# Pooling maps folded into the output projection, in a fused attention, pooling and ConvGLU block

## The reference

```python
h = rms_norm(x, norm1_g)                          # x: 2048 x 1024
q, k, v, p = split(h @ w_in)                      # 512, 128, 128, 512 columns
a = sliding_window_sink_attention(rms_norm(q), rms_norm(k), v, sinks)
for g, w in enumerate((2, 4, 8, 16)):             # four groups of 128 channels
    mixed = trailing_mean(p_g, w) - p_g           # divided by min(pos + 1, w)
    m_g = (mixed @ pool_w[g] + pool_b[g]) * pool_scale_g
x = x + concat([a, m]) @ w_out                    # 1024 x 1024
h2 = rms_norm(x, norm2_g)
u = h2 @ w_up                                     # 5632 columns
c = causal_depthwise_conv3(u) + conv_b
x = x + (silu(gate) * val) @ w_down
```

## Time and profile before

| | us |
|---|---|
| median of 3 runs | 1775.23 |
| the three runs | 1778.28, 1775.23, 1774.47 |
| the profiled execution | 1774.17 |
| its span, first to last instruction | 1772.4 |
| TensorE busy in it | 1758.5 (99%) |
| VectorE, ScalarE, GpSimd busy | 1289.6, 811.0, 251.5 |

### The profile page before, as it was taken

The page is one execution under the profiler, slowest core; times in us unless marked ns, Lnnn a source line. Parts: engine busy times, 40 slices in busy tenths (PEclk is TensorE's granted clock), DMA queues, the critical chain, the costliest instruction groups (busy, mean ns, idle before and its releaser), DMA issues.

```text
span 1772.4 us, 23447 instructions
## 1 busy us (share of the span) xinstructions
PE 1758.5 (99%) x8518; PEld 1465.8 (83%) x8518; DVE 1289.6 (73%) x1750; ACT 811.0 (46%) x1438; POOL 251.5 (14%) x272
## 2 busy tenths in 40 slices
PE   8999999999999999999999999999999999999999
PEld 7788888888878888888888888888888888888887
DVE  5645644635779888888888888888887778865774
ACT  4554644534665444444454444444444433333321
POOL 2222211202110000000000000000003033210210
PEclk9999999999999999999999999999999999999999
DMA  8653382484545524322376222223227999976884
GB/s 326 228 214 107 126 321 88 167 297 155 173 160 205 175 89 135 122 88 91 119 249 214 72 89 90 72 87 92 72 87 244 340 339 330 313 253 217 298 285 131
DMA packets 211557, 321.75 MB, mean 182 GB/s; under 512 B 13738, under 2 KB 106098, under 8 KB 211442
## 3 DMA queue, kind: packets, MB, share of 16 engines
q1 hardware_dynamic: 192014, 267.75, 45.2%
q10 hardware_dynamic: 19427, 52.49, 7.6%
HBM read 249.93 MB, written 70.25 MB: 181 GB/s over the span
## 4 chain that ended last, share of the span: by engine, by line
PE 96%; ACT 1%; DVE 1%; DMA 1%; POOL 1%; issue 0%; SPq 0%; ACTq 0%
PE ps L827 31%; PE ps L829 31%; PE ps L828 31%; PE ps L986 1%; PE ps L997 1%; PE ps L1050 1%; PE ps L1010 1%; POOL ss_q L2052 0%; DMA raw<-in_w_in_dram 0%; PE ps L973 0%; ACT xs L1251 0%; DMA x_d<-r 0%; PE ps L896 0%; DVE hT_lo L1582 0%; POOL w_lo L2074 0%
## 5 line engine op out<-in xcount | busy, mean ns | idle before, releaser
L827 PE MATMUL ps<-va_hi,wv 128*128 128x512 f32 x1232 | 479.7, 389 | 1.6 <-DVE va_lo L1769 1.4
L829 PE MATMUL ps<-va_hi,wv 128*128 128x512 f32 x1232 | 479.3, 389 | 0.0
L828 PE MATMUL ps<-va_lo,wv 128*128 128x512 f32 x1232 | 479.3, 389 | 0.0
L827 PEld LDWEIGHTS ps<-va_hi,wv 128*128 128x128 f32 x1232 | 231.3, 188 | 50.7 <-issue 2.3
L829 PEld LDWEIGHTS ps<-va_hi,wv 128*128 128x128 f32 x1232 | 231.3, 188 | 48.1
L828 PEld LDWEIGHTS ps<-va_lo,wv 128*128 128x128 f32 x1232 | 231.3, 188 | 47.7
L827 PE MATMUL ps<-dt_hi,ds_hi 128*128 128x512 f32 x616 | 239.6, 389 | 0.0
L828 PE MATMUL ps<-dt_lo,ds_hi 128*128 128x512 f32 x616 | 239.6, 389 | 0.0
L829 PE MATMUL ps<-dt_hi,ds_lo 128*128 128x512 f32 x616 | 239.6, 389 | 0.0
L1856 DVE SCALAR_TENSOR_TENSOR cb<-ub,cst,cb 128x1024 f32<-128x1024 f32 x176 | 218.9, 1286 | 9.1 <-ACT cb L1377 9.1
L1377 ACT ACTIVATE cb<-ub,cst 128x1024 f32<-128x1024 f32 x88 | 109.2, 1244 | 158.1 <-DVE ub L1905 94.6
(11 more groups left out here) (173 smaller groups left out, 2782.3 us busy)
## 6 DMA issues: line engine op xcount, KB each, us to landing
dg<-gT_d SPq DMA_DIRECT2D x264, 256.0 KB, 5.6
rw<-in_w_up_dram SPq DMA_DIRECT2D x84, 512.0 KB, 5.1
dw<-in_w_down_dram SPq DMA_DIRECT2D x132, 256.0 KB, 5.6
gT_d<-cb ACTq DMA_DIRECT2D x44, 512.0 KB, 2.6
raw<-in_w_out_dram SPq DMA_DIRECT2D x32, 512.0 KB, 4.0
w_hi<-wA_d SPq DMA_DIRECT2D x30, 512.0 KB, 3.4
w_lo<-wA_d SPq DMA_DIRECT2D x30, 512.0 KB, 4.8
n<-in_x_dram SPq DMA_DIRECT2D x16, 512.0 KB, 7.4
```

What stands on the lines that cost most here:

```text
L827: pe.matmul(out_ap, l_hi, r_hi, start=first, stop=False, skip_group_check=True)
L828: pe.matmul(out_ap, l_hi, r_lo, start=False, stop=False, skip_group_check=True)
L829: return pe.matmul(out_ap, l_lo, r_hi, start=False, stop=last, skip_group_check=True)
```

## The change

Before block 0's first `q` unit the four pool_w are turned on PE, scaled by pool_scale and split (`pwt`). Four new units `wp` in block 0 load the lower half of w_out, split it as any unit, and multiply it by the turned pool_w; ACT copies the eight 128x512 products out and stores them to DRAM (wP_d). `o` units k < 2 read wP_d in place of w_out. `pm` is gone in all blocks, with the splits in `win`. The bias row: SP loads the lower half of w_out once more into r (`bias_load`), POOL multiplies each of four rows by the bias and sums (`bias_sum`, seven passes over 128x1024), `bias_halves` splits the sum, PE sums over the partitions with a matrix of ones in block 1 (`bias`, four matmuls), ACT copies the row out (bias_all), and POOL adds it to the residual rows of every block before they are used (`rb`, four passes over 128x1024 a block). Block 0's residual rows are loaded later (`r_load`), since r holds the weights till then. The rest are orders: in blocks 1 and 2 the second `t1` part goes between `sp` 0 and 1; in the last block o(0,1) is cut into three pieces around the attention, `t2` takes other banks and waits, the second `va` loads and `va(0,2)` go later, and in up unit 0 the halves c = 0 go first, `hi(1,0)`/`lo(1,0)` go ahead, and the last `t2` pairs go into the middle of product 4.

```diff
@@ attention_order
+        if not back:
+            units("pwt", a, ())
         units("q", a, (0,))
-        units("pm", a, (0,), (1,))
+        if a == 1:
+            units("bias_halves", a, ())
         units("win", a, (2,))
...
         units("q", a, (1,))
+        if a == 1:
+            units("r_load", a, ())
         units("win", a, (3,))
         if more:
             units("n1sc", a + 1, ())
         units("q", a, (2,))
-        units("pm", a, (2,))
+        if a == 1:
+            units("bias", a, ())
+        if not back:
+            units("wp", a, (0, 0))
         units("q", a, (3,))
...
             units("t1", a + 1, (0,))
-            units("pm", a, (3,))
+            units("wp", a, (0, 1))
             units("t1", a + 1, (1,))
...
-            units("s", a, (0,), (1,))
+            units("bias_load", a, ())
+            units("s", a, (0,))
+            units("bias_sum", a, (0,))
+            units("s", a, (1,))
...
             units("inv", a, (1,))
+            units("bias_sum", a, (1,), (2,), (3,))
...
             units("av", a, (0,), (1,))
+            units("wp", a, (1, 0))
             units("sp", a, (2,), (3,))
...
             units("av", a, (2,), (3,))
+            units("wp", a, (1, 1))
             units("kve", a + 1, ())
             continue
+        units("rb", a - 1, ())
         units("o", a - 1, (0, 0), (0, 1))
...
     units("n2sq", last - 1, ())
+    units("rb", last, ())
     units("o", last, (0, 0))
     units("av", last, (0,), (1,))
-    units("o", last, (0, 1))
+    units("piece", last, (0,))
     units("sp", last, (2,), (3,))
     units("pt", last, (2,), (3,))
     units("n2sc", last - 1, ())
+    units("piece", last, (1,))
     units("av", last, (2,), (3,))
+    units("o", last, (0, 1))
     units("first_weights", last, ())
     units("t2", last - 1, (0,))
     units("o", last, (0, 2))
@@ SP
+            def r_load(a):
+                sp.wait_ge(S["bias_step"], 7)
+                sp.dma_start(r[:], x_v[:, 0:NT, :]).then_inc(r_in[0], 16)
@@ PE
+            def wp(a, n, h, pair):
...
+                for k in range(2):
+                    g = 2 * pair + k
+                    wait(pe, "fold_copied", 2 * (u - 1) + k + 1)
+                    mm = passes(ps[:, 4 + k, :], pw_hi[:, g, :], pw_lo[:, g, :], hi[:, k, :], lo[:, k, :], True, True)
...
                 if a == 1 and g < 2:
-                    pe.wait_ge(S["m_copied"], 3 + g)
+                    pe.wait_ge(S["fold_copied"], 3 + g)
...
+                        if dt < 2:
+                            pe.wait_ge(S["PT_ready"], NT * NB - 1 + dt)
+                        else:
+                            pe.wait_ge(S["aT_lo"], NT * NB - 3 + dt)
@@ ACT
             def first_weights(_):
                 act.wait_ge(S["spread_done"], NT * NB)
-                act.wait_ge(S["pool_done"], 4 * NB)
+                act.wait_ge(S["r_ready"], NT * NB)
                 for i in range(NP):
                     hi(0, i)
@@ DVE
             def o(a, n, h, k):
...
                 for t in range(NT):
+                    if h == 0:
+                        dve.wait_ge(S["r_ready"], NT * a + t + 1)
@@ POOL
+            def bias_sum(a, g):
+                total = acc[:].rearrange("p h n -> p (h n)")
+                g_.tensor_tensor(r[:, g, :] if g else total, r[:, g, :], pbias[:, g:g + 1].broadcast_to([P, D]), ALU.mult
+                                 ).then_inc(S["bias_step"], 1)
+                if g:
+                    pool.wait_ge(S["bias_step"], 2 * g)
+                    g_.tensor_tensor(total, total, r[:, g, :], ALU.add).then_inc(S["bias_step"], 1)
+
+            def rb(a):
+                if a == 0:
+                    pool.wait_ge(S["fold_copied"], BIAS_COPIED)
+                if a == NB - 1:
+                    pool.wait_ge(S["xs2"], NT * a)
+                pool.wait_ge(r_in[a % 2], 16 * (a // 2 + 1 + (a % 2 == 0)))
+                for t in range(NT):
+                    g_.tensor_tensor(rows[a][:, t, :], rows[a][:, t, :], bias_all[:].rearrange("p h n -> p (h n)"), ALU.add
+                                     ).then_inc(S["r_ready"], 1)
@@ first_up, DVE (ACT alike)
-                v_lo(1, 4)
+                v_lo(0, 4)
                 add_u2(0)
-                v_lo(0, 4)
+                v_lo(1, 4)
+                v_lo(0, 5)
                 v_lo(1, 5)
-                v_lo(0, 5)
                 add_u3(0)
                 add_c22(0)
+                v_lo(0, 6)
                 v_lo(1, 6)
-                v_lo(0, 6)
+                lo(1, 0)
```

More of the change, by code:

```diff
@@ L185 @@
 N_SPLIT = len(SPLIT_NO)
-KEPT_UNITS = [n for n in SPLIT_NO if UNITS[n][0] != "o"]
+KEPT_UNITS = [n for n in SPLIT_NO if UNITS[n][0] not in ("wp", "o")]
 def first_unit(n):
@@ L835, in halves_there, with by_token @@
                     pe.wait_ge(w_in[n % RING], halves_in(n))
-            def by_token(n, k, units, per_unit, place, left, signal, tile_wait, tiles_of_bank=1):
+            def by_token(n, k, units, per_unit, place, left, signal, tile_wait, tiles_of_bank=1, piece=None):
                 halves_there(n)
@@ L1012, in av, with piece, o @@
                 mm.then_inc(S["mix_done"], 1)
-            def o(a, n, h, k):
+            def piece(a, i):
+                o(a, UNIT["o", a, 0, 1], 0, 1, PIECES[i])
+            def o(a, n, h, k, part=None):
+                if part is None and (a, h, k) == (NB - 1, 0, 1):
+                    part = PIECES[2]
                 def tile_wait(t):
@@ L1056, in _ @@
             pe.wait_ge(const_pool, CONST_POOL)
-            walk(dict(t1=t1, pin=pin, pm=pm, kv=kv, q=q, kt=kt, qt=qt, s=s, sp=sp, av=av, o=o, t2=t2))
+            walk(dict(t1=t1, pin=pin, pwt=pwt, wp=wp, bias=bias, kv=kv, q=q, kt=kt, qt=qt, s=s, sp=sp, av=av, o=o, piece=piece, t2=t2))
             def up(un):
@@ L1197, in carry, with pwt, wp, bias_halves @@
                 a_.activation(p_keep[:, g, :], bank[:, T - CARRY:T], ACT.Copy).then_inc(S["p_copied"], 1)
-            def pm(a, g):
-                act.wait_ge(S["pool_done"], 4 * a + g + 1)
-                a_.activation(mf[:, g, :], ps[:, pm_bank(a, g), :], ACT.Identity, bias=pbias[:, g:g + 1],
-                              scale=pscale[:, g:g + 1]).then_inc(S["m_copied"], 1)
+            def pwt(a):
+                act.wait_ge(const_ready, CONST_READY)
+                act.wait_ge(S["fold_mm"], 1)
+                for g in range(4):
+                    a_.activation(pw_hi[:, g, :], ps[:, 4, tokens(g)], ACT.Copy, scale=pscale[:, g:g + 1]
+                                  ).then_inc(S["fold_hi"], 1)
+            def wp(a, n, h, pair):
+                u = folded(h, pair)
+                split(n + LEAD)
+                for k in range(2):
+                    i = 2 * u + k
+                    if k == 0:
+                        act.wait_ge(S["fold_mm"], u + 2)
+                    else:
+                        act.wait_ge(S["unit_used"], n + 1)
+                    if i == KEEP:
+                        act.wait_ge(S["fold_out"], 16 * KEEP)
+                    a_.activation(wp_kept[:, i % KEEP, :], ps[:, 4 + k, :], ACT.Copy).then_inc(S["fold_copied"], 1)
+                for k in range(2):
+                    i = 2 * u + k
+                    act.wait_ge(S["fold_copied"], i + 1)
+                    act.dma_start(wP_d[:, 2 * pair + k, h * 512:(h + 1) * 512], wp_kept[:, i % KEEP, :]
+                                  ).then_inc(S["fold_out"], 16)
+            def bias_halves(a):
+                act.wait_ge(S["bias_step"], 7)
+                act.wait_ge(S["fold_out"], 16 * 8)
+                a_.activation(acc_hi[:], acc[:], ACT.Copy).then_inc(S["fold_hi"], 1)
+            def bias(a):
+                act.wait_ge(S["fold_mm"], 6)
+                a_.activation(bias_all[:], ps[:, 4:6, :], ACT.Copy).then_inc(S["fold_copied"], 1)
             def kv(a, n, k):
@@ L1842, in va3 @@
                 v_lo(1, 3)
-            walk(dict(n1=n1_, n1sc=n1sc, t1=t1, win=win, pin=pin, pl=pl, o=o, q=q, qn=qn, kv=kv, kve=kve, join=join, s=s, inv=inv, inv1=inverse, av=av,
+            walk(dict(n1=n1_, n1sc=n1sc, t1=t1, win=win, pwt=pwt, wp=wp, bias_halves=bias_halves, pin=pin, pl=pl, o=o, q=q, qn=qn, kv=kv, kve=kve, join=join, s=s, inv=inv, inv1=inverse, av=av,
                       n2sc=n2sc, first_weights=first_weights, va=va, va3=va3))
```

181 lines of the change are left out of this document (106 added, 75 removed).

## The result

The changed kernel takes 1779.36 us (median of 8 runs, 1778.01 to 1780.98), the kernel before 1774.85 beside it (8 runs). The ratio is 1.0024, interval 1.0015 to 1.0034: slower by 4.3 us, where 3.5 less was forecast. The profiled execution has a span of 1778.0 in place of 1772.4, 5.6 more, so 5.6 + 3.5 = 9.1 us have to be found.

What follows compares the result with a forecast made beforehand. TensorE's instruction stream plus its waits was taken to bound the kernel. Terms -4.1 - 1.2 + 3.9 - 2.1 = -3.5 us against 1774.17 gave 1770.7, put at 1771.3 for timed runs; range 1765.5 to 1776.5.

Steps and rivals of the forecast that it cites:

- PE's work: TensorE's stream: 48 pm matmuls removed, wp, bias and pwt added, -4.1 us in sum; block 0 about even (+0.4).
- Block 0, waits: Block 0: three changes in TensorE's waits, together -1.2 us, bounds -1.7 to +1.8.
- (1): Block 0, q(3): its split is issued a stage later, a wait of 0.4, up to 3 if weights come late too.
- (3): Block 0, after av: two waits filled by wp matmuls vanish, -1.5 us.
- (2): Block 0, pin(1,0): the ACT and DVE chain that PE follows stands 0.7 to 0.8 later, +0.3 of waits.
- Bias on POOL: bias_sum, r_load and rb in blocks 0 to 2: hidden, held DVE splits have a unit (5.4 us) of slack; nothing.
- The last block: Last four rb passes on POOL collide with DVE's split and sums, delaying ACT and PE's o(1,0): +3.9 us.
- the 0.9 in front: Last block, reordered attention: loses two waits, -0.9, a gain ending in front of the same wait, inside the +3.9.
- Up unit 0: Up unit 0: new order removes three PE waits, -2.1 us, bounds -2.1 and -1.0; a slip at hi(1,1) returns it in full.
- A: The forecast, -3.5 us, 1769.3 to 1773.3, chance 0.5; sign: two PE waits after o(3,0,3), together about 4.8 us.
- C: Slower: late bias sum on POOL holds q(1,2)'s weights, PE loses about 8, 1779; chance 0.08; sign: weights wait there.
- D: Same as before: rb in blocks 0 to 2 costs 2 to 4, 1774, chance 0.17; sign: block 2's o under 4 earlier.

Runs made afterwards that it cites:

- 8: Changed kernel with wp(0,0) between q(1) and q(2) and wp(0,1) ahead of kv(1,0): ratio to before 1.0020.
- the best: Changed kernel, old up unit 0 order, block 3's rb in gaps, wp apart, r_load behind q(1,3)'s weights, block 0's rb behind o(0,0,3)'s split: 1770.0 us, ratio 0.9976.
- 3: Changed kernel with ACT's wait for the sixteen rb passes moved to the seventh of the first up weights only: ratio to before 1.0022.
- 4: Changed kernel with block 3's four rb passes straight behind block 2's, near 416: ratio to before 1.0006.
- 6: Changed kernel, block 3's rb in two halves, first behind DVE's maxima and ahead of inv(3,0), second behind block 2's second norm: 1772.9 us, ratio to before 0.9989.
- 1: Changed kernel with hi(1,0) on ACT back behind the last two pairs of h2 copies in up unit 0: ratio to before 1.0021.
- 2: Changed kernel with the whole old order of up unit 0 on TensorE, ACT and DVE: ratio to before 1.0016.
- 7: Changed kernel with wp(0,0) and wp(0,1) both between q(1) and q(2) of block 0: ratio to before 1.0057.
- 12: Kernel before with TensorE stalled ahead of o(3,1,0) for four small POOL operations: ratio to before 1.0045.
- 5: Changed kernel with block 3's rb in halves, tiles 0 and 1 behind inv(3,0), 2 and 3 behind the second norm: ratio to before 0.9999.
- 9: Changed kernel with old order of up unit 0, block 3's rb in halves and wp apart together: ratio to before 1.0004.

## Why the prediction was wrong, step by step

The largest term, the two waits of the last block, was right in mechanism and nearly in size. Three steps failed: the order of up unit 0, forecast as a gain of 2.1 and measured as a loss (6); the cost of a wait, taken as its length, where the lower clock behind it added 2.4 (5); and the waits of block 0 and of the bias, where late weights at pin(1,0) and two held splits were put at nothing (2, 3).

1. **PE's work, -4.1: right.** Its partition in the text was not: all of wp and pwt belongs to block 0, which by the same counts is +3.1; the +0.4 holds only up to pin(1,0). The sum is unaffected. From 276.66 to 452.14 one block's part, 2.7 by the counts, measures 3.1. In the kernel before, TensorE waits 0.35 on hT_lo at 332.64, and in the changed one this wait is gone; the order of t1 and sp had been priced at nothing. No run tests that order by itself.
2. **Block 0, waits: -1.2 forecast, +0.2 measured.** (1) No wait at q(3), in place of 0.4. (3) The two waits after av went, as forecast. (2) failed: I followed ACT and DVE into pin(1,0) and asked for late weights only at q(3). The ring has three slots, and with two short units in it pin(1,0)'s slot came free at wp(0,0)'s end; the load was issued 6.6 later than before, and its first instruction took 2.75 in place of 0.32. Moving wp(0,0) brought the issue back to 61.55 and the wait on weights away (8).
3. **Bias on POOL: nothing forecast, 1.4 measured.** The sum itself was in time, r's load is issued at 129.5. q(1,2) still waits 0.4 behind its 2 MB. And rb(0) holds two splits from 1.2 each to 6.1 together, for 1.1 at o(0,0,2), where I had counted a unit of slack (PE starts it at 167.63). Both go with the two edits of the best. DVE of the changed kernel, beside rb(0), which runs from 164.01 to 176.41:

```profile
164.69 6.13 DVE L1639 TENSOR_TENSOR w_lo<-raw,w_hi 128x1024 fp32r<-128x1024 f32 x2
```

4. **The last block, +3.9: right in place and nearly in size.** TensorE loses 5.3 from 482.74 to 484.41 where 4.8 were forecast (3.9 and the 0.9 in front). That POOL's passes beside DVE's sums are the cause, and not ACT's wait for them, is shown by 3 against 4 and 6: with ACT's wait moved TensorE still waits 1.6 and 2.9, with the passes moved both waits are gone or 0.7. The Trainium skill, SBUF — State Buffer, section "Who interferes with whom", has the rule that I used for operations with two SBUF inputs; it also says that `tensor_scalar` can use a mode with both port pairs and then contends, which I had not used. The 6.46 of n2sc in 6, against 2.73, agrees.
5. **The clock: 2.4, in no step.** I priced 4.8 us of two waits as 4.8 us. The failed step: the sum took a wait's cost to be its length. The stall alone, in the kernel before, lost 2.1 on top of its length.
6. **Up unit 0, -2.1 forecast: three waits gone, three new ones of 3.1 in sum, so +1.0; over the stretch +1.3.** I wrote that no wait would be over 0.3 and compared only low parts with PE's need. hi(1,0) waits for the landing of h2's stores (4.04 on ACT), a wait that four h2 copies covered in the old order. Its bound, "comes back in full", was too small: it came back one and a half times. The place of hi(1,0) alone accounts for 1.4 of the 3.1 (1); the rest goes with the order on DVE and TensorE (2), and the remaining 0.3 is not traced.

By size, from the table: 3.4 for up unit 0 (6), 2.4 the clock (5), 1.4 block 0 (2), 1.4 the bias (3), 0.5 the last block (4) and 0.4 behind TensorE's last matmul, less 0.3 that blocks 2 and 3 came out better than forecast between 276.66 and 482.74: the 9.1, but for rounding.

Of the signs, those of A came: both waits behind o(3,0,3), 5.0 together. So did one of C's, a wait for weights at q(1,2), but of 0.4 and not 8; and D's, since block 2's o starts 2.9 earlier (400.24 and 397.36) and not 4, and since a split in block 1 is late by 1 us. No rival had the sum.

## What to carry over

A pass on an engine that shares a port is placed by what it lies beside, not by the length of the idle time: the same four passes cost over 7 us of TensorE (lower clock included), 2, or under 1 in different places, and the sensitive neighbour was an operation of 0.17 us at the head of a chain. Where an instruction is moved ahead, list every semaphore that it waits for, and which of them its old neighbours had covered. An order that gains behind a stall may gain nothing once the stall is gone. Short units in a ring free a slot late: count the time between a unit's end and the use of its slot, not the number of units.

## What the runs showed of the hardware

- TensorE's granted clock fell to its lower level (0.50, 1.2 of 2.4 GHz) behind 6.5 us without a matmul, in every kernel with waits of 1.2 to 2.1 and 2.9 in the last block and 1.2 of work between them, and behind 3.5 in block 0 (7). On top of the waits 1.7 to 3.0 us were lost, 2.4 in the changed kernel. In the changed kernel and in 12 it had fallen before TensorE resumed. It did not fall behind the single wait of 1.9 to 2.0 near 452 (in 4, 5 and 9). Behind the wait for pin(1,0)'s weights, 2.4 in four of the kernels, it did both: the rows below are the same two microseconds of 6, then of 1, with granted clocks of 0.50 and 1.00. It fell in 5 as well and not in 2. PE resumes at 76.50 in 6 and at 76.47 in 1, and the same matmul near the end of pin(1,0) starts at 86.33 and 84.96, so the clock adds 1.3 to a wait of 2.4 in one execution and nothing in another; one profile does not price it.

```profile
78.00:80.00 2.00, 2.00 (x8) 1.74 (x7) 1.37 (x3) 0.69 (x1) 0.57 (x2) 0.50 0.94 330
```
```profile
78.00:80.00 2.00, 2.00 (x14) 1.47 (x12) 2.00 (x4) 1.24 (x2) 0.59 (x2) 1.00 0.96 381
```

- A DVE operation over 128x8 with both inputs in SBUF took 2.32 in place of 0.17 beside POOL's passes; a scaling with one input 1.6 a tile, over four tiles, in place of 0.68. Beside such passes DVE's operations with their data in PSUM kept their time: maxima over 128x1024 (1.21), and sums with one input from PSUM over 128x512 (0.69).
